# Attention and mLSTM of two transformer blocks: the quarter of the score matrix that the mask hides is no longer computed

## The reference

```python
s = jnp.where(kpos[None, :] <= qpos[:, None], s, NEG_INF)        # fox
in_window = (dist_i >= 0) & (dist_i < WINDOW)                    # swa
causal = jnp.tril(jnp.ones((CHUNK, CHUNK), dtype=bool))          # mLSTM, within a chunk
```

## Time and profile before

| what | value |
|---|---|
| median of three runs | 2571.97 us |
| the profiled execution | 2572.46 us, its span 2570.6 us |
| TensorE matmuls busy | 2289.4 us (89%) |
| VectorE busy | 1745.9 us (68%) |
| ScalarE busy | 1294.2 us (50%) |
| GpSimd busy | 253.2 us (10%) |
| mean granted TensorE clock | 0.954 |

### The profile page before, as it was taken

One profiled execution on the slowest core, in us unless ns is written; L12 is line 12 of the kernel. 1 busy time (PEld: TensorE's weight loads), 2 busy tenths in 40 slices (PEclk: granted clock), 3 DMA queues, 4 the chain that ended last, 5 costly groups with the idle time before them and its releaser, 6 DMA issues.

```text
span 2570.6 us, 47820 instructions
## 1 busy us (share of the span) xinstructions
PE 2289.4 (89%) x15056; PEld 2078.7 (81%) x15056; DVE 1745.9 (68%) x3636; ACT 1294.2 (50%) x2846; POOL 253.2 (10%) x286
## 2 busy tenths in 40 slices
PE   3887689999997699999889978799999986899998
PEld 3785579999997578888778936799999975788887
DVE  7665553888886966666643446638888869766665
ACT  3345244555455755555534554344554557555554
POOL 2000000000004910000010000000000029300000
PEclk7998789999999999999989979899999999999999
DMA  8761134555552045555334502345555530355554
GB/s 314 255 236 57 46 127 146 180 180 184 180 184 80 0 160 191 195 191 193 131 106 157 180 0 69 120 147 179 180 181 187 179 115 0 106 191 192 194 191 153
DMA packets 106071, 389.60 MB, mean 152 GB/s; under 512 B 12032, under 2 KB 12160, under 8 KB 105232
## 3 DMA queue, kind: packets, MB, share of 16 engines
q1 hardware_dynamic: 104688, 381.73, 43.5%
q10 hardware_dynamic: 992, 4.88, 0.5%
q0 software_dynamic: 320, 2.13, 0.2%
HBM read 387.64 MB, written 1.05 MB: 151 GB/s over the span
## 4 chain that ended last, share of the span: by engine, by line
PE 80%; POOL 8%; DVE 6%; ACT 3%; DMA 1%; issue 1%; SPq 0%; ACTq 0%; POOLq 0%; DVEq 0%
PE ps L539 18%; PE ps L506 16%; PE ps L501 16%; PE ps L503 16%; PE ps L543 9%; POOL scores L405 8%; DVE big L1131 1%; PE ps L618 1%; PE ps L598 1%; DMA big<-ada_in 1%; DVE act_lo L1184 1%; DVE lo L1108 1%; PE ps L608 1%; PE ps L646 1%; PE ps L495 1%
## 5 line engine op out<-in xcount | busy, mean ns | idle before, releaser
L841 ACT ACTIVATE hi<-raw 128x512 fp32r<-128x512 f32 x1356 | 776.3, 621 | 94.5 <-PE ps L506 87.0
L1108 DVE TENSOR_TENSOR lo<-raw,hi 128x512 fp32r<-128x512 f32 x844 | 553.3, 697 | 192.0 <-ACT hi L841 190.9
L501 PE MATMUL ps<-act_hi,hi 128*128 128x256 f32 x3376 | 557.7, 289 | 84.1 <-DVE act_lo L1184 43.4
L506 PE MATMUL ps<-act_hi,lo 128*128 128x256 f32 x3376 | 554.4, 287 | 27.9 <-DVE lo L1108 27.9
L503 PE MATMUL ps<-act_lo,hi 128*128 128x256 f32 x3376 | 553.0, 287 | 0.0
L501 PEld LDWEIGHTS ps<-act_hi,hi 128*128 128x128 f32 x3376 | 478.2, 197 | 90.7 <-DVE act_lo L1184 69.0
L506 PEld LDWEIGHTS ps<-act_hi,lo 128*128 128x128 f32 x3376 | 475.4, 196 | 30.8 <-DVE lo L1108 30.6
L503 PEld LDWEIGHTS ps<-act_lo,hi 128*128 128x128 f32 x3376 | 476.7, 196 | 0.0
L866 ACT ACTIVATE big<-ps 128x256 f32 (+1 forms) x354 | 136.2, 385 | 589.3 <-PE ps L506 589.3
L1378 DVE TENSOR_TENSOR lo<-raw,hi 128x512 fp32r<-128x512 f32 x512 | 329.1, 688 | 135.4 <-ACT hi L841 129.2
L539 PE MATMUL ps<-hi,act_hi 128*128 128x512 f32 x1024 | 398.7, 389 | 0.0
(11 more groups left out here) (180 smaller groups left out, 1371.8 us busy)
## 6 DMA issues: line engine op xcount, KB each, us to landing
raw<-u SPq DMA_DIRECT2D x256, 512.0 KB, 3.3
raw<-v SPq DMA_DIRECT2D x256, 512.0 KB, 3.4
raw<-front SPq DMA_DIRECT2D x166, 512.0 KB, 3.3
big<-ada_in SPq DMA_DIRECT2D x48, 512.0 KB, 5.5
big<-biasA_in ACTq DMA_DIRECT2D x1, 2048.0 KB, 11.1
xT<-xT_in ACTq DMA_DIRECT2D x1, 1024.0 KB, 9.7
big<-keys_in ACTq DMA_DIRECT2D x1, 1024.0 KB, 14.4
scores<-memT_in POOLq DMA_DIRECT2D x1, 1024.0 KB, 5.3
```

The lines of the kernel that those rows point to most:

```text
L501: pe.matmul(out_ap, hi_l(k), hi_r(k), start=(first and k == 0), stop=False, skip_group_check=True)
L506: mm = pe.matmul(out_ap, lo_l(k), hi_r(k), start=False, stop=(last and k == n - 1), skip_group_check=True)
L841: act.activation(hi[:, s, :, :], raw[:, rs, 4 * h:4 * h + 4, :], ACT.Copy).then_inc(hi_done, 1)
L1108: dve.tensor_tensor(lo[:, s, :, :], raw[:, rs, 4 * h:4 * h + 4, :], hi[:, s, :, :].bitcast(F32), ALU.subtract).then_inc(lo_done, 1)
```

## The change

Query tile 0 now computes with the first 128 keys alone, for all items but `mem`; query tile 1 and `mem` keep all 256. In PSUM and in `att_pt` the transposed weights are packed: key tile 0 takes 256 columns, key tile 1 only 128. In the mLSTM, key tile 1 is computed only with queries 128 to 255. The selects on GpSimd touch only the blocks on the diagonal (and, for `swa`, the block below it).

```diff
+        def seen(kind, qt):
+            return T if kind == "mem" or qt else P
+        def key_parts(kind):
+            whole = kind == "mem"
+            return [(0, 0, T, 0)] + [(1, 0 if whole else P, T if whole else P, T)]
...
-                    v = biasA[64 * half:64 * half + 64, :, qt, :]
-                    link(select(v, [[0, 8], [-1, T]], limit - 1, 0, NEG))
+                    v = biasA[64 * half:64 * half + 64, :, qt, 0:seen("a", qt)]
+                    link(select(v, [[0, 8], [-1, seen("a", qt)]], limit - 1, 0, NEG))
...
-                select(mls_w[:, h % 2, :, :], [[-P, QT], [1, T]], 0, -1, 0.0).then_inc(m_mask, 1)
+                diag = mls_w[:, h % 2, 0:2 * T].rearrange("p (a t) -> p a t", a=2)[:, :, 0:P]
+                select(diag, [[0, 2], [1, P]], 0, -1, 0.0).then_inc(m_mask, 1)
...
-            link(select(biasS, [[0, 8], [P, QT], [-1, T]], 0, 1, NEG))
-            link(select(biasS, [[0, 8], [-P, QT], [1, T]], P - 1, -1, NEG))
+            for qt in range(QT):
+                link(select(biasS[:, :, qt, qt * P:qt * P + P], [[0, 8], [-1, P]], 0, 1, NEG))
+            link(select(biasS[:, :, 1, 0:P], [[0, 8], [1, P]], -1, -1, NEG))
             pool.wait_ge(fox_d, 1)
-            link(select(biasF, [[0, 8], [P, QT], [-1, T]], 0, 1, NEG))
+            for qt in range(QT):
+                link(select(biasF[:, :, qt, qt * P:qt * P + P], [[0, 8], [-1, P]], 0, 1, NEG))
...
+        def mls_part(h, st):
+            return mls_w[:, h % 2, st * T:st * T + T - st * P]
...
-                        mm = pe.matmul(bx[i % 2][:, qt * T:qt * T + T], a["q"][:, P * qt:P * qt + P], a["k"],
-                                       start=True, stop=True)
+                        n = seen(ITEMS[i][0], qt)
+                        mm = pe.matmul(bx[i % 2][:, qt * T:qt * T + n], a["q"][:, P * qt:P * qt + P],
+                                       a["k"][:, 0:n], start=True, stop=True)
-                    for kt in range(QT):
-                        for qt in range(QT):
-                            mm = pe.transpose(bx[2][:, kt * T + qt * P:kt * T + qt * P + P],
+                    for kt, t0, n, at in key_parts(ITEMS[i][0]):
+                        for qt in range(t0 // P, QT):
+                            mm = pe.transpose(bx[2][:, at + qt * P - t0:at + qt * P - t0 + P],
-                        mm = pe.matmul(bo[i % 2][0:a["dh"], :], a["v"](kt),
-                                       att_pt[:, i % 2, kt, :], start=(kt == 0), stop=(kt == QT - 1))
+                        mm = pe.matmul(bo[i % 2][0:a["dh"], t0:t0 + n], a["v"](kt),
+                                       att_pt[:, i % 2, at:at + n], start=(kt == 0), stop=(kt == QT - 1))
...
-                    pe.matmul(bx[h % 2][:, st * T:st * T + T], qkc[:, 4 + h, st * P:st * P + P], qkc[:, h, :],
-                              start=True, stop=True)
+                    pe.matmul(bx[h % 2][:, st * T:T + st * P], qkc[:, 4 + h, st * P:st * P + P],
+                              qkc[:, h, st * P:T], start=True, stop=True)
-                    pe.matmul(o[:, 0:T], vb[:, st, h * P:h * P + P], mls_w[:, h % 2, st, :], start=(st == 0),
+                    pe.matmul(o[:, st * P:T], vb[:, st, h * P:h * P + P], mls_part(h, st), start=(st == 0),
-                    mm = pe.matmul(o[:, T:2 * T], ones[:, :], mls_w[:, h % 2, st, :], start=(st == 0),
+                    mm = pe.matmul(o[:, T + st * P:2 * T], ones[:, :], mls_part(h, st), start=(st == 0),
```

More of the change, by code:

```diff
@@ L201, in two_blocks_kernel @@
         att_s = cut(27136, 3, QT, T)
-        att_pt = cut(30208, 2, QT, T)
+        att_pt = cut(30208, 2, QT * T)
         rstd = cut(31232, 2, T)
         keysA = cut(21536, 16, P)
-        mls_w = cut(23584, 2, QT, T)
+        mls_w = cut(23584, 2, QT * T)
         vT1 = cut(23584, 4, T)
@@ L906, in exps @@
                     for qt in range(QT):
-                        ins = act.activation(att_s[:, i % 3, qt, :], att_s[:, i % 3, qt, :], ACT.Exp,
-                                             bias=sm[:, qt:qt + 1], scale=-1.0, accum_out=sm[:, 2 + qt:3 + qt])
+                        s = att_s[:, i % 3, qt, 0:seen(ITEMS[i][0], qt)]
+                        ins = act.activation(s, s, ACT.Exp, bias=sm[:, qt:qt + 1], scale=-1.0,
+                                             accum_out=sm[:, 2 + qt:3 + qt])
                     ins.then_inc(att["e"], 1)
@@ L914, in copy @@
                         act.wait_ge(att["o"], i - 1)
-                    act.activation(att_pt[:, i % 2, :, :].rearrange("p a t -> p (a t)"), bx[2], ACT.Copy)\
-                        .then_inc(att["c"], 1)
+                    n = sum(part[2] for part in key_parts(ITEMS[i][0]))
+                    act.activation(att_pt[:, i % 2, 0:n], bx[2][:, 0:n], ACT.Copy).then_inc(att["c"], 1)
                 exps(first)
@@ L1010, in _ @@
                 act.wait_ge(m_d, h + 1)
-                w = mls_w[:, h % 2, :, :]
+                w = mls_w[:, h % 2, 0:T + P]
                 act.activation(w, w, ACT.Exp, scale=-1.0).then_inc(m_e, 1)
@@ L1208, in bias_max @@
                     for qt in range(QT):
-                        bias = zeros[:, :] if a["bias"] is None else a["bias"][:, qt, :]
+                        n = seen(ITEMS[i][0], qt)
+                        bias = zeros[:, :] if a["bias"] is None else a["bias"][:, qt, 0:n]
                         start = 3e38 if a["sink"] is None else neg_sinks[:, a["sink"]:a["sink"] + 1]
-                        ins = dve.tensor_tensor_reduce(out=att_s[:, i % 3, qt, :], in0=bx[i % 2][:, qt * T:qt * T + T],
+                        ins = dve.tensor_tensor_reduce(out=att_s[:, i % 3, qt, 0:n], in0=bx[i % 2][:, qt * T:qt * T + n],
                                                        in1=bias, scale=-a["scale"], scalar=start, op0=ALU.add,
@@ L1223, in normalise @@
                     for qt in range(QT):
-                        ins = dve.tensor_scalar(att_s[:, i % 3, qt, :], att_s[:, i % 3, qt, :], sm[:, 6 + qt:7 + qt],
-                                                None, ALU.mult)
+                        s = att_s[:, i % 3, qt, 0:seen(ITEMS[i][0], qt)]
+                        ins = dve.tensor_scalar(s, s, sm[:, 6 + qt:7 + qt], None, ALU.mult)
                     ins.then_inc(att["p"], 1)
@@ L1436, in exponents @@
                 for st in range(QT):
-                    ins = dve.tensor_scalar(mls_w[:, h % 2, st, :], bw[h % 2][:, 0:T], g_col[:, st, h:h + 1], 0.0,
+                    ins = dve.tensor_scalar(mls_part(h, st), bw[h % 2][:, st * P:T], g_col[:, st, h:h + 1], 0.0,
                                             ALU.subtract, ALU.max)
@@ L1442, in weighted @@
                 dve.wait_ge(m_mask, h + 1)
-                w = mls_w[:, h % 2, :, :].rearrange("p a t -> p (a t)")
-                dve.scalar_tensor_tensor(out=w, in0=bx[h % 2], scalar=P ** -0.5, in1=w, op0=ALU.mult, op1=ALU.mult)\
+                w = mls_w[:, h % 2, 0:T + P]
+                dve.scalar_tensor_tensor(out=w, in0=bx[h % 2][:, 0:T + P], scalar=P ** -0.5, in1=w, op0=ALU.mult, op1=ALU.mult)\
                     .then_inc(m_w, 1)
```

## The result

The changed kernel took 2575.4 us (median of 20 runs, 2572.49 to 2580.51). The kernel before, run beside it, took 2569.76 us (median of 20, 2564.57 to 2577.52). The ratio is 1.0019, with a 95% interval of 1.0012 to 1.0027. The change makes the kernel slower by 0.2%, less than 0.3% and clear of noise, where 17 us faster was forecast. The mean granted clock separates the kernels: it is 0.941 to 0.943 in all twenty executions of the changed kernel, while of 52 executions of the kernel before that ran beside the first experiments 47 had 0.953 to 0.955 and took 2564.35 to 2572.54 us, and five had 0.950 or 0.951 and took 2574.91 to 2577.34 us.

A forecast was written before the change was run, and what follows sets the result against it. Mostly TensorE in the dense stages was taken to bound the kernel; savings of 4.6 + 8.5 + 2.6 + 1.75 = 17.4 us in the attentions, mLSTM and selects gave 2555 us, range 2548 to 2563 us.

The forecast's parts named there:

- The step that failed: Both attentions: the stretch at clock 0.50 keeps its length, 10.9 us in block 1 and 12.0 us in block 2.
- The first rival: Attentions: the clock gate doesn't raise the clock or lets it fall, so items stay at half clock; chance 0.15.
- its first case: Attentions: the clock gate costs five to sixteen items, giving 2563 to 2579 us; chance 0.10.
- its second case: Attentions: the clock gate costs more than five to sixteen items; chance 0.05.
- The rule from the Trainium skill: Attentions: clock swings because TensorE idles a little between groups of matmuls; cited as The first rival's mechanism, no size.
- TensorE's price: Attention items: 0.11 us per shortened instruction, 0.145 per dropped transpose, 0.585 us an item at full clock.
- The loop over three engines: Attentions: the two-item loop loses 0.925 us; items take 2.13 us (`a`, `fox`) and 2.38 (`swa`) at full clock.
- The second rival: VectorE-ScalarE handoffs don't shorten, only TensorE's part is saved, 0.29 us an item: 2559.5 us; chance 0.14.
- The sum: Whole kernel: attentions 4.6 and 8.5, mLSTM 2.6, selects 1.75, together 17.4 us saved.
- mLSTM and selects: mLSTM's two pairs of heads save 2.6 us; block 1's shorter GpSimd selects save VectorE's `ada` steps 1.75 us.
- The third rival: Attentions: the clock rises earlier, each half-clock part giving up to 4.7 us more, down to 2546 us; chance 0.07.

The follow-up runs named there:

- m6: The changed kernel plus one value product of 128 columns per masked item, result not read: 2561.49 us, ratio 0.997.
- m1: The changed kernel with both score products of TensorE at 256 columns again, the extra 128 never read: 2587.08 us, ratio 1.0069.
- w2: The changed kernel plus dense products: nine before block 1's first transposes, twelve before block 2's attention, nine in its wait for first exponentials: 2543.9 us, ratio 0.9905.
- m2: The changed kernel with four transposes, the 512-column copy and 256-column value products again for every item: 2561.7 us, ratio 0.997.
- m5: The changed kernel plus a fourth transpose per masked item, result not read: 2565.09 us, ratio 0.9983.

## Why the prediction was wrong

- **The step that failed** is "I keep the half-clock part at 10.9 us, since TensorE is without a rest in it before and [...] after", and the same with 12.0 us in block 2. TensorE was without a rest after the change, and the clock did not rise. The half-clock part lasted the scores of all sixteen masked items of block 2 (50.4 us) and the whole attention of block 1. Being busy was not enough; what TensorE was given to do counted: 0.43 us more an item brought the rise back in block 2 as a value product (m6), 0.42 us more as whole scores didn't (m1). The runs that put TensorE's work back (2561.7, 2561.02 us) and those that raised the clock from outside (2543.9 us) show it from both sides.
- **The rival had the mechanism.** The first rival named the gate, and 2575.4 us lies in its first case (2563 to 2579), but that is partly luck: this case held five to sixteen items at half clock, and of the items that the forecast had at full clock some 18 ran at half (5.1 + 4.8 + 8). By the rival's own prices that is 27.4 us, or 2582 us, in its second case. I gave it 0.15, on the strength of the window with 85% busy at a clock of 0.98. That row says that a risen clock holds, as w2 confirmed at 14.49 of 16.00 us in `swa`. It says nothing about whether the clock rises. The rows that did bear on it were the 10.9 and 12.0 us of unbroken work at half clock, which I wrote down as "no strong case" and then didn't weigh. The price that the rival gave for block 2, 28.6 us over the forecast, was too high: attention 2 was forecast 8.5 us shorter and came out 9.2 longer, 17.7 us. It took the `mem` items at half clock (9.6 us), which ran at 0.99.
- **The rule from the Trainium skill.** The Trainium skill (TensorE: Matmul & The Clock Gate, section "A second HAM failure mode: psum-queue depth-cycling") speaks of a clock that swings when TensorE idles a little between groups. That isn't what happened: there were no idle gaps in the 50.4 us at 0.50 in block 2, and no swing.
- **TensorE's price.** Right. At full clock four instructions of `s` went from 1.06 to 0.85 and of `o` from 1.01 to 0.80, which is 0.105 for each shortened one (0.11 taken). The dropped transpose was worth 0.10 and not 0.145, since part of a group's time belongs to no single transpose: 0.58 for four, 0.48 for three. At half clock an item came to 3.88 us, 3.77 forecast.
- **The loop over three engines.** Right. 2.16 and 2.405 us an item against 2.13 and 2.38. The second rival, that waits take over, falls: it wanted `swa` above 2.5.
- **The sum.** With the clock held in both kernels the change gives 16.7 us. My terms at full clock throughout, 8 x 0.52 + 0.1 = 4.3 in block 1, 8 x 0.52 + 8 x 0.46 + 0.3 = 8.1 in block 2, 2.6 and 1.75, make 16.8. That the two agree so closely is luck: 16.7 is known to some 5 us, and the stages of the two traces give 3.97, 7.41, 0.90 and 1.70, together 14.0.
- **mLSTM and selects.** 2.33 us against 2.6 and 1.70 against 1.75. In the mLSTM the path was not the one that I had forecast, so the near match is in part luck. I had the scores of one head only on the chain in the second pair. After the change the chain passes those of both heads, at half clock with their broadcasts (7.25 us from 280.01 to 287.26), and one division of the first pair in place of two. The sums of the first pair ran at full clock (0.92 and 0.67; 1.17 and 1.72 before). With the burst in both kernels the clock lay differently again, and the mLSTM gave 0.90 us.
- **The third rival**, an earlier rise, didn't come in the changed kernel. Its price was a little low for block 2: 3.18 items at 1.64 us are 5.2 us and not 4.7.

## What to carry to other kernels

Before trimming TensorE's work, look at how the granted clock got to where it is in that stage. If it rose only after long unbroken work, less work may cost more time than it saves: here about a quarter less gave +9.2 us in one attention. A handful of dense products on free operands, placed in a wait right ahead of the stage, costs little there (first scores to first transposes of block 2 took 4.70 us in w2 and 3.46 in w1, both at full clock) and turned 0.2% slower into 1.0% faster; it must reach up to the first real product, as the burst that stood too early showed. When two changes of this kind are judged, give both kernels the burst, else the clock can decide and not the change.

## What the runs showed of the hardware

- A clock of 0.50 lasted 50.4 us with TensorE busy 50.40 of 50.40 us. The dense fp32r products behind attention 1 had full clock back 3.1 us (m2), 3.6 us (kernel before), 4.1 us (changed kernel) and 5.8 us (m5) after they began; attention's float32 items after 6 to 23 us or not at all.
- Transposes seem to count for something: one more an item, and nothing else changed, brought the rise into block 2 (at 1538.9 us). How much each kind counts (rows, columns, products, transposes) stays open; whole scores of 64 rows (0.42 us more an item at half clock) didn't do it, a value product over 128 rows at about the same cost (0.43 us) did, in block 2 of the traced execution.
- GpSimd's select lengthens VectorE's two-input reduction as if the two took turns: an `ada` step of 1.13 us took 2.02 beside a select of 1024 columns and 2.88 beside one of 2048, that is 0.89 and 1.75 us more.
